# Prompt attention of a hybrid decoder step: the low part's product with the values moved one tile further behind the turning than the high part's

## The reference, cut to what matters

```python
def one_block(start):
    qb = lax.dynamic_slice_in_dim(q, start, Q_BLOCK, axis=1)
    ...
s_c = einsum('btgid,bngd->btgin', qg, kc) * scale - sl * dist_c     # 63 compressed rows
p_c = masked_softmax(s_c, mask_c); o_c = einsum('btgin,bngd->btgid', p_c, vc)
s_s, p_s, o_s = the same over the selected rows (all earlier rows here: 16 blocks of 64)
s_w, p_w, o_w = the same over the last 512 rows and the current ones
o = g[..., 0:1] * o_c + g[..., 1:2] * o_s + g[..., 2:3] * o_w
```

## Time and profile before

| | |
|---|---|
| time before, median of 3 runs | 2194.12 us (2191.2 to 2201.19) |
| the profiled execution's own time | 2199.8 us |
| its span from the first to the last instruction | 2197.8 us |
| busy in the span: PE, PEld, DVE, ACT, POOL | 2024.2, 1873.2, 1045.1, 761.8, 525.7 us |
| the prompt attention in the trace | about 515 to 831 us from the span's start |
| one batch's tiles in it | 3 to 14; 148 in 16 batches |

### The profile page before, as it was taken

The page is one execution under the profiler, slowest core; times in us unless marked ns, Lnnn a source line. Parts: engine busy times, 40 slices in busy tenths (PEclk is TensorE's granted clock), DMA queues, the critical chain, the costliest instruction groups (busy, mean ns, idle before and its releaser), DMA issues. The chain is left out here.

```text
span 2197.8 us, 33297 instructions
## 1 busy us (share of the span) xinstructions
PE 2024.2 (92%) x13868; PEld 1873.2 (85%) x13868; DVE 1045.1 (48%) x1761; ACT 761.8 (35%) x1432; POOL 525.7 (24%) x440
## 2 busy tenths in 40 slices
PE   6999999876888986998899999899999999999997
PEld 6999999865666763565799989899999999999997
DVE  6888762456887873214232243533333323322222
ACT  4323323534766761212322232322222224432212
POOL 2444321204654562222011112111111001211000
PEclk9999999876999987999999999999999999999998
DMA  6455431101000006454433331323333333332332
GB/s 206 138 172 174 157 119 32 40 6 39 1 1 20 1 1 225 123 165 134 154 92 92 93 97 44 96 87 90 94 88 87 95 106 92 105 104 87 87 90 66
DMA packets 258148, 203.12 MB, mean 92 GB/s; under 512 B 20342, under 2 KB 237276, under 8 KB 252687
## 3 DMA queue, kind: packets, MB, share of 16 engines
q1 hardware_dynamic: 246399, 150.92, 23.6%
q0 software_dynamic: 6144, 39.46, 5.3%
q10 hardware_dynamic: 5456, 10.62, 1.5%
HBM read 178.59 MB, written 26.54 MB: 93 GB/s over the span
## 5 line engine op out<-in xcount | busy, mean ns | idle before, releaser
L2997 DVE TENSOR_TENSOR ffn_w_l<-ffn_raw,ffn_w_h 128x1024 fp32r<-128x1024 f32 (+1 forms) x136 | 163.9, 1206 | 273.7 <-ACT ffn_w_h L2930 273.4
L98 PE MATMUL banks<-h_h,ffn_w_l 128*128 128x264 f32 x1408 | 287.2, 285 | 5.5 <-DVE ffn_w_l L2997 5.5
L98 PE MATMUL banks<-h_h,ffn_w_h 128*128 128x264 f32 x1408 | 288.2, 286 | 0.0
L98 PE MATMUL banks<-h_l,ffn_w_h 128*128 128x264 f32 x1408 | 287.2, 285 | 0.0
L2930 ACT CAST ffn_w_h<-ffn_raw 128x1024 fp32r<-128x1024 f32 (+1 forms) x136 | 138.6, 1021 | 331.5 <-PE banks L98 330.4
L98 PEld LDWEIGHTS banks<-h_h,ffn_w_l 128*128 128x128 f32 x1408 | 220.4, 189 | 6.0 <-DVE ffn_w_l L2997 5.8
L98 PEld LDWEIGHTS banks<-h_h,ffn_w_h 128*128 128x128 f32 x1408 | 219.4, 189 | 0.0
L98 PEld LDWEIGHTS banks<-h_l,ffn_w_h 128*128 128x128 f32 x1408 | 218.8, 189 | 0.0
L2918 POOL TENSOR_TENSOR act_l_rest<-ffn_act,act_h 128x528 fp32r<-128x528 f32 x38 | 71.5, 1883 | 375.8 <-ACT act_h L2938 375.8
L89 PE MATMUL banks<-fm_hT_h,fm_w_l 128*128 128x352 f32 x648 | 147.3, 336 | 1.4 <-DVE hT_l L918 1.4
L680 POOL TENSOR_TENSOR fm_w_l<-fm_raw,fm_w_h 128x512 fp32r<-128x512 f32 x54 | 95.1, 1762 | 220.8 <-ACT fm_w_h L754 220.7
(11 more groups left out here) (522 smaller groups left out, 4264.9 us busy)
## 6 DMA issues: line engine op xcount, KB each, us to landing
ffn_raw<-in_w_ffn_in_dram SPq DMA_DIRECT2D x88, 512.0 KB, 3.8
ffn_raw<-in_w_ffn_out_dram SPq DMA_DIRECT2D x32, 512.0 KB, 4.0
fm_raw<-in_w_in_dram SPq DMA_DIRECT2D x44, 256.0 KB, 3.1
early_w_raw<-in_w_in_dram SPq DMA_DIRECT2D x32, 256.0 KB, 3.0
merge_raw<-in_w_in_dram SPq DMA_DIRECT2D x32, 256.0 KB, 2.9
ffn_raw<-in_w_ffn_out_dram SPq DMA_DIRECT2D x16, 384.0 KB, 3.5
hT_copy<-fm_hT_h SPq DMA_DIRECT2D x4, 1056.0 KB, 5.3
hT_copy<-hT_l SPq DMA_DIRECT2D x4, 1056.0 KB, 5.3
```

The costliest lines, as they stand in the source:

```text
L98: mm = pe.matmul(out[:, bank, 0:cols.stop - cols.start], w[:, kt, :], x[:, cols], start=(first and n == 0), stop=(last and n == 2))
L2997: dve.tensor_tensor(w_l[n % NSPLIT][:, 0:m, :], raw[n % NRAW][:, 0:m, :], w_h[n % NSPLIT][:, 0:m, :].bitcast(F32), ALU.subtract).then_inc( ...
```

## The change

The products of the high and the low part are split into two functions, and the low part's is issued one tile later. In slot x PE now issues the high part's product of tile x-2 and the low part's of tile x-3. No instruction is added or taken away, and ACT, DVE and POOL have the same instructions in the same order. The waits stand with the products to which they belong. The semaphore `s_pv`, which counts finished tiles, is still raised by the low part's product.

```diff
+            def pv_high(x):
+                b, n, (_, _, _, m) = tiles[x]
                 if n == 0 and b:
                     pe.wait_ge(s_out, b)
                 if x == 0:
                     pe.wait_ge(s_vl, 3 * NG)
                 pe.wait_ge(s_ph, x + 1)
+                pe.matmul(ps[:, 7, :], value_of(x), pt_h[x % NPT][0:m, :], start=(n == 0), stop=False)
+
+            def pv_low(x):
+                b, _, (_, _, _, m) = tiles[x]
                 pe.wait_ge(s_pl, x + 1)
+                pe.matmul(ps[:, 7, :], value_of(x), pt_l[x % NPT][0:m, :], start=False, stop=(x + 1 == first_tile[b + 1]))\
                   .then_inc(s_pv, 1)
...
                 turn(x)
                 if x > LAG and tiles[x - LAG - 1][1] == 0:
-                    pv(x - LAG - 1)
-                if x >= LAG and tiles[x - LAG][1]:
-                    pv(x - LAG)
+                    pv_high(x - LAG - 1)
+                if x > LAG and tiles[x - LAG][1] == 0:
+                    pv_low(x - LAG - 1)
+                elif x >= LAG and tiles[x - LAG][1]:
+                    pv_high(x - LAG)
+                    if x > LAG:
+                        pv_low(x - LAG - 1)
             for x in range(first_tile[NBAT - 1], len(tiles)):
-                pv(x)
+                pv_high(x)
+                if tiles[x][1]:
+                    pv_low(x - 1)
+            pv_low(len(tiles) - 1)
```

More of the change, by code:

```diff
@@ L1817, in turn, with value_of @@
                 mm.then_inc(s_turn, 1)
-            def pv(x):
-                b, n, (branch, kt, _, m) = tiles[x]
+            def value_of(x):
+                b, _, (branch, kt, _, m) = tiles[x]
                 g, _ = batches[b]
+                return vc_hl[g][0:m, :] if branch == CMP else v_hl[g][:, branch, kt, :]
+            def pv_high(x):
+                b, n, (_, _, _, m) = tiles[x]
                 if n == 0 and b:
@@ L1825, in pv @@
                     pe.wait_ge(s_vl, 3 * NG)
-                v = vc_hl[g][0:m, :] if branch == CMP else v_hl[g][:, branch, kt, :]
                 pe.wait_ge(s_ph, x + 1)
-                pe.matmul(ps[:, 7, :], v, pt_h[x % NPT][0:m, :], start=(n == 0), stop=False)
+                pe.matmul(ps[:, 7, :], value_of(x), pt_h[x % NPT][0:m, :], start=(n == 0), stop=False)
+            def pv_low(x):
+                b, _, (_, _, _, m) = tiles[x]
                 pe.wait_ge(s_pl, x + 1)
-                pe.matmul(ps[:, 7, :], v, pt_l[x % NPT][0:m, :], start=False, stop=(x + 1 == first_tile[b + 1]))\
+                pe.matmul(ps[:, 7, :], value_of(x), pt_l[x % NPT][0:m, :], start=False, stop=(x + 1 == first_tile[b + 1]))\
                   .then_inc(s_pv, 1)
```

## The result

Six runs of the changed kernel have their median at 2215.32 us (2208.31 to 2222.78), six of the kernel before beside them at 2197.8 (2191.2 to 2201.19). The ratio is 1.0078, with an interval of 1.0056 to 1.0099: slower by 0.8%. A second comparison, with six runs against 23, gives 2210.5 against 2195.88 us and 1.0071 (1.0051 to 1.0091). None of the changed kernel's first six runs lies within 3 us of their median: three are at 2208 to 2212 us and three at 2218 to 2223. Over all twelve the median is 2211.7 us. The profiled execution of the changed kernel took 2218.35 us.

A forecast was written before the change was run, and what follows sets the result against it. It took DVE and ACT together to set the pace, PE mattering only where a batch begins. The terms 10.0 - 2.6 + 1.85 + 3.2 - 0.75 = +11.7 us, laid on 2194.1, gave 2206 us, range 2190 to 2212.

The forecast's parts named there:

- What bounds the kernel: In the changed stage DVE and ACT together set the pace; PE matters only where a batch begins.
- the middle of a batch: In a batch's middle and end, one product of 0.34 us leaves the path to turning; taken as 0 gain.
- The cost at the beginning: Seven batch beginnings (1 to 5, 12, 13): `out_part` delayed to start of F+2's turning + 1.05; together +10.0 us.
- Batch 2: At batch 2's beginning, the rule for the late copy gave a loss of 1.51 us.
- The gain at batches 6 to 11: Scores computed during PE's former wait: batches 7 to 9 gain, -2.6 us; 6, 10 and 11 still lose, +1.85 us.
- The last two: Beginnings of batches 14 (lower clock, +2.2) and 15 (+1.0): the copy comes later, together +3.2 us.
- What PE gives back: In the middles of batches 7 to 9, three short waits of ACT for a turning go: -0.75 us.
- The row change: Separated 63-row products cost PE some 0.4 us more in each of 16 batches; bounds 0 to 6 us, taken as 0.
- The first (turning sets the pace): Rival: each of 46 waits for the low part gives 0.34 us, stage faster, 2178.5 us; chance 0.10.
- the second (delays absorbed): Rival: DVE's slack behind ACT eats up the delays at batch beginnings, 2190 to 2200 us; chance 0.25.
- The third, the clock falling more often: Rival: the heads of batches 7 to 9 stay cold and three more fall, 2214 us; chance 0.10.
- The rule of the skill: No full clock for transposes: thirteen batches' turning-to-product step 0.36 us longer, about 4.7 us more; left out of the sum.

The follow-up runs named there:

- the second profile: The changed kernel, unaltered, timed and profiled again against the kernel before: 2210.5 us, ratio 1.0071; its profiled execution took 2209.89 us, stage 328.4 us.
- the later copy: The changed kernel with `out_part` and `out_sum` one slot later on ACT and DVE: 2196.05 us, ratio 0.9995 to the kernel before.
- the dose: The changed kernel with a batch's last low product still in slot F+2, but ahead of the turning: 2206.53 us, ratio 1.0036 to the kernel before.
- the last product in place: The changed kernel with only a batch's last low product put back to slot F+1: 2197.11 us, ratio 1.0001 to the kernel before.
- The second profile of the kernel before: The kernel before, unaltered, one more profiled execution: stage 315.6 us.
- The first profile: The changed kernel's first profiled execution, nothing else altered: 2218.35 us, stage 331.9 us.

## Why the prediction was right and wrong

**What bounds the kernel: right.** DVE and ACT together set the pace. Their work is the same to 0.2 us and the stage grew by what both wait at a batch's beginning. Taking 0 for the middle of a batch was right too: PE waits 34 us less ahead of the low product (and 18 us more ahead of turnings), and the distances are those of the heads' delays. (The 6.0 us for which DVE waited for scores are L1913's alone; the other score line, L1924, has 2.7 us more in 5 places. It changes nothing in the sum.)

**The cost at the beginning: right in rule and size.** "Start of F+2's turning + 1.05" holds within 0.02 us in batches 5 and 7 of the profile after, and within 0.07 at every head that ran at the full clock, in all five profiles. At the lower clock the distance is 1.82 to 1.88 us. Batches 3, 4, 5, 12 and 13 come out within 0.07 us of their terms in the second profile, which has the full clock in all of them, and batch 1 within 0.2. (Two of these terms are not what the subtraction gives: from the rows, batch 3 is 1.38 and batch 12 is 1.22. And in batch 1 PE's first turning did not wait for DVE, as the prediction says of all seven: it stood right behind its scores, at the lower clock.) That it acts through the copy in two queues is shown by the later copy (0.9995) and by the dose.

**Batch 2: wrong, 1.5 us too much.** The delay is there (the copy waits 1.44 us). But before, that head ran partly at the lower clock, in both profiles, and with the change in none of five. These rows of before stand in no group above; the turning takes 0.76 us and a product of 128 rows 0.78:

```profile
552.75 0.76 PE L1815 MATMUL banks<-ident,scores 128*128 128x128 f32 x4 [2.64 <-DVE scores L1953]
553.16 0.78 PE L1828 MATMUL banks<-probsT_h,values_hl 128*128 128x512 f32 x1
```

What the rule adds, the clock gives back. The step that failed here was to price the head by one trace's rows without asking which level of the clock the changed kernel would have there. Why the clock is up there in the change stays open.

**The gain at batches 6 to 11: right.** Forecast -2.6 and +1.85, measured -2.25 and +2.30 in the second profile. The clock does stay up at batches 7 to 9 in all five profiles, DVE's wait for scores fell from 6.0 to 1.8 us, and with the last product in place the same batches give 1.9 us each. (The second profile of the kernel before has batch 9's head at the full clock and a longer dip in batch 8; its batches 7 to 9 together are 0.2 us shorter, so the base of this gain holds.)

**The last two: mis-sized.** +3.2 was forecast; measured 5.5 in three profiles, 1.2 and 2.5 in the others. The term took one clock for batch 14. At the lower one its copy waits 3.63 us, at the full one 1.37, and both occur. At the lower one the copy starts 1.84 us behind the turning's start, and the term had taken 1.65.

**What PE gives back: wrong.** The 0.75 us in the middles of batches 7 to 9 did not come; their distances are 0.1 us each above the forecast, not below. ACT's waits for PE in the middles of batches 7 and 9 (0.26 and 0.34 us before) are gone in the second profile, but the time is not: a shorter wait of ACT was not a shorter batch.

**The row change: 0 was right.** The product of 63 rows does take 0.50 us in its new place, as before, and with the later copy, which has every such change, batches 5 and 10 to 12 are within about 0.3 us of before's. A cost of 0.4 us in each batch that the stage had to bear would be seen there; one that PE's waits cover would not.

**The rivals.** The first (turning sets the pace) and the second (delays absorbed) are refuted by nearly every distance in the table. The third, the clock falling more often, was real in part. Its three cold heads, batches 7 to 9, came up as forecast. But batch 3 fell in three of five profiles, and batch 14 was down in three of five and up in two, both down only in the first. It had a chance of 0.10 as a case apart, and some head outside the forecast's terms at another level is a part of each of the five.

**Why 2215.3 and not 2206.** Of the 9.5 us (from 2205.8), 3.7 are the base: the sum was laid on 2194.1, the median of three runs, and six runs gave 2197.8. The remaining 5.8 are 11.7 forecast against 17.5. The profiles' stages show +13.5 in three of five, +14.9 and +16.9. In the second profile the 1.8 us above the forecast are -1.5 (batch 2), +2.3 (batches 14 and 15), +0.8 (batches 6 to 11), +0.75 (nothing given back), and -0.6 in small ones with the stage's end. That +13.5 is so near +11.7 is in part luck, since misses of opposite sign cancel. What the profiles leave of the 17.5, 0.6 to 4 us, is scatter ahead of the stage or is not explained; the median of twelve runs, 2211.7, leaves less.

**The step that failed.** The prediction priced each head at one level of the clock, as the single trace of before had it or as one was counted on, and put the other level into rival 3 instead of into the terms. Batches 3 and 4 were to cost 2.8 us: they cost 2.8 at the full clock, and 6.5 to 7.2 in the three profiles in which batch 3's head was at the lower one. Batches 14 and 15 were to cost 3.2: they cost 5.5, or 1.2 to 2.5 where batch 14's head was at the full clock. The first profile, the only one with both at the lower level, has its +16.9 from that. The width that the forecast was given names the row change, the step from product to copy and absorption, but not the clock, and not the base, although the three runs shown spread over 10 us.

**The rule of the skill.** Four turns take 0.60 us where the clock is 1.00 and 1.11 where it is 0.50 in the profile after too. The Trainium skill (TensorE: Matmul & The Clock Gate, Part 4: PE-mode transpose) says that transposes don't get the full clock. Here they do, and the 4.7 us that the rule would have added at the heads with the clock up are not in their distances. These turns stand between products; whether turning alone would bring the clock up, no run here shows.

## What to carry to other kernels

Before an instruction is moved back, look up who reads its result and what stands behind that reader in its own in-order queue: 15 moved products, one for each batch's beginning, made the whole loss, since a copy placed early in two queues waited for them. Where a producer is delayed, move its reader by the same amount, and measure the pair together: each alone cost 0.4 to 0.7% here, and both together nothing measurable. Apply a reordering only to the iterations whose trace shows the wait that it removes, four of 16 batches here.

## What the runs showed of the hardware

The granted clock behind one and the same wait of PE (1.78 to 1.82 us ahead of batch 3) was 0.50 for 10 to 14 us in three profiles of a kernel and 1.00 in two. In the same five profiles batch 14's head, some 240 us later, was at the full clock twice, both times after a low stretch in batch 3, and at the lower one three times, once after such a stretch and twice without. So a row at a batch's head tells its price for one clock only, and two profiles of the same kernel can put 3 us in different places. Over the 51 runs of the kernel before made beside the experiments, the time falls by 1.4 us for each 0.001 of mean clock between 0.953 and 0.961; the change's twelve runs lie 11 to 18 us above that line at their own clocks (four of them, at 0.949 to 0.952, beyond its end), which says again that the clock is not most of what the change costs.
